# Dilated attention: when ScalarE squares the convolution's deviations, and when it runs the convolution's SiLU

## The reference, cut to what matters

```
s = jnp.where(valid, s + bias, -jnp.inf)                  # attention, per head and block
p = jnp.exp(s - logsumexp(s));  o = p @ v
...
z = conv(z, dw_w) + dw_b                                  # convolution, 256 channels
mu = jnp.mean(z, axis=-1, keepdims=True)
var = jnp.mean(jnp.square(z - mu), axis=-1, keepdims=True)
z = (z - mu) * lax.rsqrt(var + CONV_LN_EPS) * ln_w + ln_b
return jax.nn.silu(z)
```

## Time and profile before

| what | value |
|---|---|
| median of 3 runs | 3479.65 us (3474.78 to 3480.0) |
| the profiled execution | 3479.74 us, its span 3478.0 us |
| PE busy | 3328.0 us, 96% |
| DVE, ACT, POOL busy | 1747.1, 1274.5, 336.6 us |
| dilated attention, layer 1 | from 637.8 to 693.4 us of the span |
| dilated attention, layer 2 | from 1710.7 to 1765.4 us of the span |

### The profile page before, as it was taken

One profiled execution on the slowest core, in us unless ns is written; L12 is line 12 of the kernel. 1 busy time (PEld: TensorE's weight loads), 2 busy tenths in 40 slices (PEclk: granted clock), 3 DMA queues, 4 the chain that ended last, 5 costly groups with the idle time before them and its releaser, 6 DMA issues. The chain is left out here.

```text
span 3478.0 us, 52375 instructions
## 1 busy us (share of the span) xinstructions
PE 3328.0 (96%) x21106; PEld 2732.5 (79%) x21106; DVE 1747.1 (50%) x2634; ACT 1274.5 (37%) x1871; POOL 336.6 (10%) x277
## 2 busy tenths in 40 slices
PE   7999999799999999999889999988999998899998
PEld 5888879588888888878778888876888875578886
DVE  4443365564444444355464443556665354666642
ACT  3222356642223222345652222434222232542221
POOL 0000325400000000042500000010000002400000
PEclk9999999899999999999989999999999998999999
DMA  3233320032332223220022232312333240022232
GB/s 113 96 98 106 107 73 4 16 99 97 96 104 89 97 96 107 96 93 25 15 67 97 96 101 93 128 55 79 96 96 105 101 178 4 13 85 97 96 102 80
DMA packets 73607, 295.75 MB, mean 85 GB/s; under 512 B 8160, under 2 KB 9056, under 8 KB 72288
## 3 DMA queue, kind: packets, MB, share of 16 engines
q1 hardware_dynamic: 73440, 293.32, 25.5%
HBM read 291.19 MB, written 2.10 MB: 84 GB/s over the span
## 5 line engine op out<-in xcount | busy, mean ns | idle before, releaser
L441 PE MATMUL bank<-src_hi,tile_hi 128*128 128x512 f32 x2736 | 1078.9, 394 | 26.5 <-DVE tile_lo L522 25.7
L443 PE MATMUL bank<-src_hi,tile_lo 128*128 128x512 f32 x2736 | 1065.7, 389 | 0.0
L442 PE MATMUL bank<-src_lo,tile_hi 128*128 128x512 f32 x2736 | 1065.3, 389 | 0.0
L522 DVE TENSOR_TENSOR tile_lo<-raw_tiles,tile_hi 128x1024 fp32r<-128x1024 f32 (+1 forms) x486 | 625.8, 1311 | 84.7 <-ACT tile_hi L471 68.2
L441 PEld LDWEIGHTS bank<-src_hi,tile_hi 128*128 128x128 f32 x2736 | 514.1, 188 | 146.5 <-DVE tile_lo L522 26.1
L442 PEld LDWEIGHTS bank<-src_lo,tile_hi 128*128 128x128 f32 x2736 | 514.3, 188 | 112.1 <-issue 6.7
L443 PEld LDWEIGHTS bank<-src_hi,tile_lo 128*128 128x128 f32 x2736 | 514.0, 188 | 107.6
L471 ACT ACTIVATE tile_hi<-raw_tiles 128x1024 fp32r<-128x1024 f32 (+1 forms) x486 | 526.6, 1112 | 77.5 <-DMA raw_tiles<-in_b_in 33.2
L441 PE MATMUL bank<-hid_hi,tile_hi 128*128 128x512 f32 x1312 | 514.3, 392 | 25.4 <-DVE tile_lo L522 25.4
L442 PE MATMUL bank<-hid_lo,tile_hi 128*128 128x512 f32 x1312 | 513.2, 391 | 0.0
L443 PE MATMUL bank<-hid_hi,tile_lo 128*128 128x512 f32 x1312 | 512.8, 391 | 0.0
(11 more groups left out here) (338 smaller groups left out, 3168.7 us busy)
## 6 DMA issues: line engine op xcount, KB each, us to landing
raw_tiles<-in_gu SPq DMA_DIRECT2D x264, 512.0 KB, 3.5
raw_tiles<-in_down SPq DMA_DIRECT2D x96, 704.0 KB, 4.1
raw_tiles<-in_w_in SPq DMA_DIRECT2D x46, 512.0 KB, 3.5
raw_tiles<-in_a_in SPq DMA_DIRECT2D x17, 512.0 KB, 3.5
raw_tiles<-in_w_out SPq DMA_DIRECT2D x16, 512.0 KB, 3.6
raw_tiles<-in_w_mem SPq DMA_DIRECT2D x16, 512.0 KB, 3.5
masks<-in_masks SPq DMA_DIRECT2D x4, 1948.0 KB, 8.3
raw_tiles<-in_b_in SPq DMA_DIRECT2D x9, 512.0 KB, 3.6
```

Source lines behind the costliest of these rows:

```text
L441: nc.tensor.matmul(bank, wh, hi[:, kk, 0:p.n], start=(kk == 0), stop=False)
L442: nc.tensor.matmul(bank, wh, lo[:, kk, 0:p.n], start=False, stop=False)
L443: mm = nc.tensor.matmul(bank, wl, hi[:, kk, 0:p.n], start=False, stop=last and (p.kind == "gated" or s == p.h - 1))
L522: v.tensor_tensor(self.tile_lo[:, t, 0:kc * P], self.tile_raw[:, t, 0:kc * P], self.tile_hi[:, t, 0:kc * P].bitcast(F32), ALU.subtract).th ...
```

## The change

The squares move from `finish_activations` at step 2, which comes after the exponentials and copies of that step, into a function of their own that is called at the head of step 2, ahead of the third unit's exponentials. PE waits for both centred tiles ahead of its waits for the squares. The SiLU is done in step 9 (the tenth), after that step's exponentials and copies, and not in step 13.

```
                 for s in range(n + 2):
+                    if finish and s == 2:
+                        self.finish_squares(act, own)
                     if s < n:
...
         if s == 3:
+            pe.wait_ge(own["conv_centred"], CV)
             for c in range(CV):
                 pe.wait_ge(own["conv_squared"], c + 1)
...
+    def finish_squares(self, act, own):
+        _, acc, _ = self.conv_memory()
+        for c in range(CV):
+            act.wait_ge(own["conv_centred"], c + 1)
+            self.nc.scalar.activation(self.units("h", c, 1)[:, 0, :], acc[:, c, :], ACT.Square).then_inc(own["conv_squared"], 1)
...
-        if s == 2:
-            for c in range(CV):
-                act.wait_ge(own["conv_centred"], c + 1)
-                nc.scalar.activation(self.units("h", c, 1)[:, 0, :], acc[:, c, :], ACT.Square).then_inc(own["conv_squared"], 1)
...
-        if s == n + 1:
+        if s == 9:
             for c in range(CV):
                 act.wait_ge(own["conv_normed"], c + 1)
                 nc.scalar.activation(acc[:, c, :], acc[:, c, :], ACT.Silu, bias=self.p1("cln_b", c))
```

## The result

The changed kernel takes 3485.18 us (median of 20 runs), the kernel before 3477.59 us in the same comparison: ratio 1.0021, 95% interval 1.0014 to 1.0028, so 7.6 us slower. One of the 20 executions, 8587.9 us, stands apart from the other 19 (3479.57 to 3488.02), moves the median by 0.2 us, is not in the ratio, and nothing here explains it. The profiled execution took 3482.84 us, its span is 3481.1 us. A second comparison gave 1.0021 again (1.0011 to 1.0031).

The account below looks back on a forecast made before the run. TensorE, busy 3328.0 of 3478.0 us, bounds the kernel, except in two dilated attention phases where engines wait in a ring. Layer 1 +0.5, layer 2 +0.95 and clock 1.6 gave +3.0: 3482.6 us, range 3474.5 to 3489.

Parts of the forecast that it names:

- no change: Whole kernel: a time within about 0.2% (7 us) of before, given a chance of 0.80.
- slower by over 0.2%: Whole kernel: a time above 3486.6 us, given a chance of 0.16.
- The squares: Step 3, before the variance products: PE's idle 1.40 us (layer 2: 0.51) goes, worth -0.7 and -0.25 us.
- The added wait: PE's wait on the centred values before the variance products: between 0 and 51 ns, taken as 0.
- The SiLU in the tenth step: ACT, steps 9 to 11: two table loads and two SiLUs, 3.89 us less 1.38 slack, +2.4 us per layer.
- The end: End of each dilated attention phase: without load and SiLUs, DVE's copy ends it, -1.2 us per layer.
- The clock after the gap: PE after its new idle gap near 684: low clock may last longer, bounds -3.2 to +3.8, taken as +0.8 us per layer.
- rival A: Gap near 684 spreads the low clock through the next stretch and into w_out: 5.5 us per layer, 3492 us; chance 0.14.
- Where the clock falls: Dilated attention phases: each fall to 0.50 was said to follow PE going idle for two or three microseconds.
- Rival C: ACT drains at each of two table switches, 1.09 us each, +4.4 over both layers: 3487.0 us; chance 0.05.
- Rival D: Other work hides PE's lag on ACT, leaving only gains from end and squares: 3476.3 us; chance 0.10.
- Rival B: Closing step 3's gap returns the clock sooner or skips a fall, up to -3.2 per layer: 3474.7 us; chance 0.19.

Follow-up runs that it names:

- e1: Changed kernel with the SiLU put back at the last step, so only the squares and added wait differ from the kernel before: 3477.1 us, ratio 0.9996 to before.
- e1b: Repeat run of the kernel with the squares alone moved and the SiLU at the last step: 3474.5 against 3479.22 us for the kernel before, ratio 0.9985.
- e8: Kernel before with only the SiLU moved, one tile each into the twelfth and thirteenth step, squares where they were: 3472.54 us, ratio 0.9984 to before.
- e3: Changed kernel with one SiLU each in the twelfth and thirteenth step, after the last exponentials, squares early: 3470.52 us, ratio 0.9977 to the kernel before.
- e2: Changed kernel with the squares put back where the kernel before has them, SiLU still in the tenth step: 3486.45 us, ratio 1.0023 to before.
- e4: Changed kernel with SiLU in the tenth step replaced by Identity with the same bias, needing no table load: 3470.88 us, ratio 0.9978 to before.
- e5: Changed kernel with six products that nothing reads put into PE's gap at the twelfth step: 3485.37 us, ratio 1.0018 to the kernel before.

## Why the prediction was right, and where its sizes were off

The measured 3485.18 us lies in the range, and the places of the sum are where it put them. The size is not: +3.0 was forecast, +7.6 measured. That is at the bound between "no change" and "slower by over 0.2%", and the second had only a chance of 0.16. That the time came out only 2.6 us above the forecast 3482.6 is in part luck: the forecast starts from a median of three runs, 3479.65, and the median of 20 is 2.1 us lower.

- *The squares*: the idle time went, nothing behind them was late. The value of -0.7 and -0.25 came from a clock that would return at the old moment. It did not: the lows of the earlier trace rows from 648.30 lasted 6.85 us, the new one, from about 648.4, ended near 651.75, in this profile. In layer 1 of the second profile it lasted 6.8 us again. The worth over both layers is 2 to 3 us with the SiLU late (0.10% in the mean of e1 and e1b, 0.07% between e8 and e3) and under 1 us with the SiLU in the tenth step (e2 beside the changed kernel), against 0.95 in the sum.
- *The added wait*: nothing, as the run with the squares and the wait alone shows.
- *The SiLU in the tenth step*: 3.9 us of ACT less 1.38 us of slack; forecast 2.4, measured 2.34 on ACT. PE's idle time was that long (2.14 to 2.35 us) where PE came to it at half clock, as in the kernel before, and 3.34 us where it came at full clock. The load of the exponentials' table came as forecast.
- *The end*: DVE's copy sets it. But 1.2 us per layer is too little a price: e8 gained 5.6 us with nothing but that. The gap ahead of `w_out` falls from 5.10 to 3.92 us; that the clock gives the rest is argued, not shown.
- *The clock after the gap* is the term that was mis-sized. It was put at +0.8 per layer, with rival A's +5.5 as the far end. The terms without it are 2 x 2.34 for the SiLU, -0.7 to -3 for the squares and -2.4 (or, by e8, -5.6) for the end, in all +1.6 to -3.9; the sizes from medians hold a share of the clock themselves. Measured were +7.6. So the clock behind the gap makes 3 to 6 us per layer. Two other estimates agree: e4 has 15 us for 5.1 us of loads, so 10 us or 5 per layer, and e5 gives some 3.5 per layer. The mechanism was rival A's, in both layers of both profiles and in one layer of e2, and its price, 5.5 per layer, was near. What misled was the argument against it, that PE has work on both sides of the gap. Why the clock did not come back on that work is not shown. In the changed kernel 3.4 us of PE's work without idle time stood behind the gap (683.72 to 687.17), then groups with 0.74 and 0.56 us of idle time between them, and the clock stayed low. In layer 2 of e2 the same work stood there, and the clock was back 3.0 us into it.
- *Where the clock falls*: "each fall comes after PE had gone idle for two or three microseconds" does not hold for the last fall of either phase. In layer 1 PE's last product ended at 691.05 + 0.44 = 691.49 and the clock fell at 692.70, after 1.2 us.
- *Rival C*, a drain at each switch, is out. "ScalarE: Activation LUTs" in the Trainium skill, section "What ACT_TABLE_LOAD costs", adds about 1.38 us to every load. The trace does not agree: here SiLU starts 0.02 us after its load ends, and the load 0.02 after the copy. The same page of the Trainium skill, section "Rules for kernel authors", advises to finish one set before switching. This case agrees: breaking the rule added two loads, 2.6 us of ACT, and the kernel is 7.6 us slower.
- *Rival D*, a hidden delay, is out by PE's idle 3.34 us. *Rival B*'s cause, an earlier return of the clock at step 3, did take place in three of the four phases of the two profiles, and the SiLU's gap outweighed it.

## What to carry to other kernels

In a ring of engines where PE works directly behind ACT, price a delay by what it does to TensorE's clock and not only by its length: here a microsecond of table load cost three. Put a function of another table after the last use of the table that it displaces, in a wait of ACT that the trace shows. Products that nothing reads, put into PE's gap, did keep the long low away, but what overruns the gap gives the gain back: price them by a row of the same shape at both clocks (here 1.99 and 3.59 us for two). Moving the SiLU out of the tenth step gained far more than filling its gap.

## What the hardware showed that was not expected

A low can outlast much work: PE was busy 8.48 of 15.35 us between 682.55 and 697.90 of the changed kernel and stayed at 0.50, while 3.35 us of PE without a gap from 648.40 were followed by full clock. Nor is it only scattered work that a low outlasts. This one of the kernel before went on for 6.8 us with PE busy for nearly all of them:

```profile
665.40:672.20 6.80, 6.54 (x38) 5.11 (x38) 4.23 (x12) 3.63 (x13) 2.55 (x2) 0.50 0.01 2
```

And the clock stayed at 1.00 from 685.85 to 692.70 with 3.81 us of PE's work in 6.85. Executions of one kernel lie 12 us apart (3471.25 to 3482.92 for the kernel before). The same phase took 56.6 us in layer 1 and 53.3 us in layer 2 of one profile of e1, where it had four lows in layer 1 and three in layer 2. A single pair of profiles (3478.0 and 3481.1 us of span) had shown less than half of the difference of the medians.
